# Retention of a two-block transformer layer: centred values, early scores and states, squares on ScalarE, decays inside the stick attention

## The reference

```python
scores = einsum('bhnid,bhnjd->bhnij', qc, kc) * dmat
inner = einsum('bhnij,bhnjd->bhnid', scores, vc)
kv = einsum('bhnjd,bhnje->bhnde', kc * k_dec, vc)
# state n+1 = g_chunk * state n + kv_n, from zero
cross = einsum('bhnid,bhnde->bhnie', qc, state) * q_dec
y = inner + cross
mu, var = mean(y), mean((y - mu) ** 2)      # over the 64 columns of a head
out = ((y - mu) * rsqrt(var + EPS) * gain + bias) * silu(r_g)
```

## Time and profile before

| | us |
|---|---|
| median of 3 runs | 2454.27 (2451.46 to 2454.89) |
| the profiled execution | 2452.69 |
| its span | 2450.8 |

### The profile page before, as it was taken

One profiled execution on the slowest core, in us unless ns is written; L12 is line 12 of the kernel. 1 busy time (PEld: TensorE's weight loads), 2 busy tenths in 40 slices (PEclk: granted clock), 3 DMA queues, 4 the chain that ended last, 5 costly groups with the idle time before them and its releaser, 6 DMA issues.

```text
span 2450.8 us, 30913 instructions
## 1 busy us (share of the span) xinstructions
PE 2273.3 (93%) x10560; PEld 1837.1 (75%) x10560; DVE 1862.5 (76%) x2142; ACT 1397.5 (57%) x1644; POOL 162.9 (7%) x106
## 2 busy tenths in 40 slices
PE   5998888999998998667899999999999999999988
PEld 3866676888787885655588888888888888878866
DVE  7887535556424757565699999999999999999975
ACT  4355524333314336204477778777777778778763
POOL 1000000000000000001001101110110111011010
PEclk8999798999999998678799999999999999999999
DMA  9520313332113210216799999999999999999990
GB/s 326 193 104 14 108 36 102 103 101 79 53 61 116 91 50 1 95 48 242 251 379 375 374 382 375 375 381 375 375 375 381 375 375 381 375 375 377 379 340 35
DMA packets 286881, 571.96 MB, mean 233 GB/s; under 512 B 10556, under 2 KB 35039, under 8 KB 286783
## 3 DMA queue, kind: packets, MB, share of 16 engines
q1 hardware_dynamic: 273615, 523.69, 58.7%
q0 software_dynamic: 13200, 47.38, 6.9%
HBM read 542.71 MB, written 28.32 MB: 233 GB/s over the span
## 4 chain that ended last, share of the span: by engine, by line
PE 57%; SPq 26%; DVE 8%; issue 4%; ACT 3%; DMA 2%; DVEq 0%; ACTq 0%; POOL 0%
SPq L800 25%; PE bank L1793 6%; PE bank L1794 6%; PE bank L1795 6%; PE bank L1443 6%; PE bank L1444 6%; PE bank L1445 6%; PE bank L1642 3%; PE bank L1643 3%; PE bank L1644 3%; PE bank L1424 3%; PE bank L1521 2%; PE bank L1503 1%; SPq L652 1%; DMA x<-in_x 1%
## 5 line engine op out<-in xcount | busy, mean ns | idle before, releaser
L2473 DVE TENSOR_TENSOR w_lo<-stage,w_hi 128x2048 fp32r<-128x2048 f32 x396 | 885.4, 2283 | 5.8 <-ACT w_hi L1258 5.8
L1258 ACT ACTIVATE w_hi<-stage 128x2048 fp32r<-128x2048 f32 x396 | 753.8, 1920 | 197.0 <-DMA stage<-in_w_down 80.4
L1793 PE MATMUL bank<-w_hi,xeT_hi 128*128 128x512 f32 x1056 | 439.2, 416 | 0.0
L1794 PE MATMUL bank<-w_lo,xeT_hi 128*128 128x512 f32 x1056 | 413.3, 391 | 0.0
L1795 PE MATMUL bank<-w_hi,xeT_lo 128*128 128x512 f32 x1056 | 413.3, 391 | 0.0
L1795 PEld LDWEIGHTS bank<-w_hi,xeT_lo 128*128 128x128 f32 x1056 | 199.4, 189 | 42.6
L1794 PEld LDWEIGHTS bank<-w_lo,xeT_hi 128*128 128x128 f32 x1056 | 199.9, 189 | 40.6
L1793 PEld LDWEIGHTS bank<-w_hi,xeT_hi 128*128 128x128 f32 x1056 | 200.5, 190 | 37.4
L1793 PE MATMUL bank<-w_hi,eaT_hi 128*128 128x512 f32 x528 | 209.0, 396 | 4.6 <-DVE eaT_lo L2518 4.6
L1954 DVE TENSOR_TENSOR ring_low<-ring,half_top 128x2048 fp32r<-128x2048 f32 (+2 forms) x42 | 93.1, 2221 | 151.0 <-ACT half_top L994 150.6
L1794 PE MATMUL bank<-w_lo,eaT_hi 128*128 128x512 f32 x528 | 206.1, 390 | 0.0
(11 more groups left out here) (468 smaller groups left out, 3596.4 us busy)
## 6 DMA issues: line engine op xcount, KB each, us to landing
stage<-in_w_up_gate SPq DMA_DIRECT2D x264, 1024.0 KB, 14.0
stage<-in_w_down SPq DMA_DIRECT2D x132, 1024.0 KB, 17.6
ring<-in_w_ada SPq DMA_DIRECT2D x12, 2048.0 KB, 9.4
ring<-in_w_up SPq DMA_DIRECT2D x22, 1024.0 KB, 7.7
ring<-in_w_in SPq DMA_DIRECT2D x10, 2048.0 KB, 7.8
ring<-in_w_out SPq DMA_DIRECT2D x4, 2048.0 KB, 12.8
ring<-in_w_down SPq DMA_DIRECT2D x4, 2048.0 KB, 8.5
stage<-in_w_ple_gate SPq DMA_DIRECT2D x4, 1024.0 KB, 14.5
```

The source lines that it names most:

```text
L1258: fn(w_hi[top_of(h)][:, :], src[:, :], ACT.Copy).then_inc(s_hi, 1)
L1793: mm(bank[b][:, :], hi[:, kk, :], wh[:, k, :], start=bcol is None and kk == 0, stop=False)
L1794: mm(bank[b][:, :], hi[:, kk, :], wl[:, k, :], start=False, stop=False)
L2473: tt(w_lo[h][:, :], stage[h][:, :], w_hi[top_of(h)][:, :].bitcast(FP), ALU.subtract).then_inc(s_lo, 1)
```

## The change

`rv` is centred: each head's mean over its 64 columns is subtracted from the values as soon as they are there, ahead of the stick attention; since outputs and states are linear in the values, the retention's output then has mean zero in each head, and the norm's copy, mean and subtraction go. The off-diagonal zeros of the state come from GpSimd, ahead. The eight decays move from ahead of the stick attention into its steps 1 to 8 on VectorE. There are two tiles of `rS`, three of `state`, two of `gy` and `gsq`. TensorE makes scores two chunks ahead and the key-value products one chunk ahead. ScalarE squares the output straight from the bank. The gain row is multiplied into the gate and the bias row times the gate becomes `gadd`, one chunk ahead (`ret_gate`), so the norm multiplies twice and adds once. ScalarE's two halves of `top` for `wout2` are taken apart, one in chunk 1 and one in chunk 2.

```diff
@@ -215,10 +215,11 @@
+    rS = [at(R + (80 + 6 * i) * KB, [P, H, P], name=f"rS{i}") for i in range(2)]
+    state = [at((24 + 2 * i) * KB, [P, H // 2, 2 * HD], name=f"state{i}") for i in range(3)]
+    gy = [at(R + (20 + 18 * i) * KB, [P, H, HD], name=f"gy{i}") for i in range(2)]
+    gadd = [at(R + (22 + 14 * i) * KB, [P, CW], name=f"gadd{i}") for i in range(2)]
+    gsq = [at(R + (32 + 2 * i) * KB, [P, H, HD], name=f"gsq{i}") for i in range(2)]
@@ -492,13 +493,21 @@
+    def scores_of(n):
+        for j in range(2):
+            product(("rS", n, j), (5 + j) if n % 2 else j)
+    scores_of(0)
+    product(("rkv", 0), 4)
+    scores_of(1)
     for n in range(NT):
-        product(("rS", n, 0), 0); product(("rS", n, 1), 1)
         product(("rO", n), 2 + n % 2)
-        if n < NT - 1:
-            product(("rkv", n), 4)
+        if n < 2:
+            product(("rkv", n + 1), 4)
         if n:
             product(("oT", 3, n - 1), 7)
+        if n < 2:
+            scores_of(n + 2)
@@ -870,6 +879,10 @@
+            full(pool, ("win2", 5, NT - 1))
+            for st in state:
+                for par in range(2):
+                    nc.gpsimd.memset(st[par * HD:(par + 1) * HD, :, (1 - par) * HD:(2 - par) * HD], 0.0).then_inc(s_kz, 1)
@@ -1222,12 +1235,26 @@
+            def ret_square(n):
+                b = full(act_e, ("rO", n))
+                if n >= 2:
+                    act_e.wait_ge(s_ms, 8 + n)
+                fn(gsq[n % 2][:, :, :], b[:, :].rearrange("p (h d) -> p h d", h=H), ACT.Square).then_inc(s_rsq, 1)
+            def ret_root(n):
+                act_e.wait_ge(s_ms, 10 + n)
+                st = hs[:, (9 + n) * 32:(9 + n) * 32 + H]
+                fn(st, st, ACT.Sqrt).then_inc(s_rt, 1)
             for n in range(NT):
-                roots(9 + n)
+                ret_square(n)
                 if n:
                     out_T(3, n - 1)
-                if n == 1:
-                    top(("wout2", 0), 0, 1)
+                ret_root(n)
+                if n in (1, 2):
+                    top(("wout2", 0), n - 1)
@@ -1679,36 +1706,51 @@
-            pe.wait_ge(s_kd, 1)
-            pe.wait_ge(s_rqd, NT)
-            for n in range(NT):
-                c0 = n * P
+            def ret_scores(n):
                 for j in range(2):
                     b = acquire(("rS", n, j))
                     for h in range(j, H, 2):
-                        ins = mm(b[:, h // 2 * P:(h // 2 + 1) * P], half(rT[1], h, c0, P), half(rT[0], h, c0, P), start=True, stop=True)
+                        ins = mm(b[:, h // 2 * P:(h // 2 + 1) * P], half(rT[1], h, n * P, P), half(rT[0], h, n * P, P), start=True, stop=True)
                     publish(ins, ("rS", n, j))
+            def ret_pairs(n):
+                b = acquire(("rkv", n))
+                for j in range(4):
+                    ins = mm(b[:, j * P:(j + 1) * P], rk[:, n, j * P:(j + 1) * P], rv[:, n, j * P:(j + 1) * P], start=True, stop=True)
+                publish(ins, ("rkv", n))
+            def ret_out(n):
                 b = acquire(("rO", n))
                 for j in range(2):
                     taken(pe, ("rS", n, j))
                 if n:
-                    pe.wait_ge(s_st, n)
+                    taken(pe, ("rkv", n - 1))
                 for pair in range(H // 2):
                     if n:
-                        mm(b[:, pair * P:(pair + 1) * P], rqdT[:, pair, c0:c0 + P], state[:, pair, :], start=True, stop=False,
+                        mm(b[:, pair * P:(pair + 1) * P], rqdT[:, pair, n * P:(n + 1) * P], state[n - 1][:, pair, :], start=True, stop=False,
                            skip_group_check=True)
                     for h in (2 * pair, 2 * pair + 1):
-                        ins = mm(b[:, h * HD:(h + 1) * HD], rS[:, h, :], rv[:, n, h * HD:(h + 1) * HD], start=n == 0, stop=True,
+                        ins = mm(b[:, h * HD:(h + 1) * HD], rS[n % 2][:, h, :], rv[:, n, h * HD:(h + 1) * HD], start=n == 0, stop=True,
                                  skip_group_check=True)
                 publish(ins, ("rO", n))
-                if n < NT - 1:
-                    b = acquire(("rkv", n))
-                    for j in range(4):
-                        ins = mm(b[:, j * P:(j + 1) * P], rk[:, n, j * P:(j + 1) * P], rv[:, n, j * P:(j + 1) * P], start=True, stop=True)
...
+            pe.wait_ge(s_kd, NT)
+            pe.wait_ge(s_rqd, NT)
+            pe.wait_ge(s_kz, 10)
+            ret_scores(0)
+            ret_pairs(0)
+            ret_scores(1)
+            for n in range(NT):
+                ret_out(n)
+                if n < 2:
+                    ret_pairs(n + 1)
                 if n:
                     out_T(3, n - 1, o2)
+                if n < 2:
+                    ret_scores(n + 2)
@@ -2378,72 +2420,107 @@
+            for t in range(NT):
+                taken(dve, ("win2", 5, t))
+            rvh = rv[:, :, :].rearrange("p t (h d) -> p (t h) d", d=HD)
+            vmean = hs[:, 4 * 32:5 * 32]
+            link(ve.reduce_sum(vmean, rvh, axis=AX))
+            link(ts(vmean, vmean, 1.0 / HD, None, ALU.mult))
+            link(tt(rvh, rvh, bc(vmean, 2, [P, 32, HD]), ALU.subtract))
             for t in range(NT):
                 full(dve, ("rT", 1, t))
             rk3 = rk[:, :, :].rearrange("p t (h d) -> p t h d", h=H)
             for t in range(NT):
                 taken(dve, ("rT", 0, t))
-                link(tt(rk3[:, t], rk3[:, t], bc(cb("kdec"), 2, [P, H, HD]), ALU.mult))
-                tt(rqdT[:, :, t * P:(t + 1) * P], rT[0][:, :, t * P:(t + 1) * P], blk3(cb("qdec")), ALU.mult).then_inc(s_rqd, 1)
-            dve.wait_ge(s_rqd, NT)
-            dve.nop().then_inc(s_kd, 1)
...
+            def while_sticking(s):
+                if 1 <= s <= NT:
+                    t = s - 1
+                    tt(rk3[:, t], rk3[:, t], bc(cb("kdec"), 2, [P, H, HD]), ALU.mult).then_inc(s_kd, 1)
+                elif NT < s <= 2 * NT:
+                    cols_t = slice((s - NT - 1) * P, (s - NT) * P)
+                    tt(rqdT[:, :, cols_t], rT[0][:, :, cols_t], blk3(cb("qdec")), ALU.mult).then_inc(s_rqd, 1)
+            attention(2, PR2, PT2, o2, while_sticking)
             dmat = cb("dmat").rearrange("p (h i) -> p h i", h=H)
-            for n in range(NT):
+            def ret_mask(n):
                 for j in range(2):
                     label = ("rS", n, j)
                     b = full(dve, label)
-                    if n:
-                        full(dve, ("rO", n - 1))
+                    if n >= 2:
+                        full(dve, ("rO", n - 2))
                     else:
                         full(dve, ("T", 2, 4 * H - 1))
-                    take(tt(rS[:, j::2, :], blk3(b[:, :]), dmat[:, j::2, :], ALU.mult), label)
-                if n < NT - 1:
-                    label = ("rkv", n)
-                    b = full(dve, label)
...
+                    take(tt(rS[n % 2][:, j::2, :], blk3(b[:, :]), dmat[:, j::2, :], ALU.mult), label)
+            def ret_state(n):
+                label = ("rkv", n)
+                b = full(dve, label)
+                if n:
+                    taken(dve, ("rkv", n - 1))
+                for par in range(2):
+                    hp = slice(par * HD, (par + 1) * HD)
+                    src = blk3(b[:, :])[hp, :, par * HD:(par + 1) * HD]
+                    own = state[n][hp, :, par * HD:(par + 1) * HD]
+                    if n == 0:
+                        ins = ve.tensor_copy(own, src)
+                    else:
+                        link(tt(own, state[n - 1][hp, :, par * HD:(par + 1) * HD], bc(cb("gch")[hp, :], 2, [HD, 4, HD]), ALU.mult))
+                        ins = tt(own, src, own, ALU.add)
+                take(ins, label)
+            def ret_gate(n):
+                link(tt(gadd[n % 2][:, :], rg[:, n, :], gnrow[:, 1, :], ALU.mult))
+                link(tt(rg[:, n, :], rg[:, n, :], gnrow[:, 0, :], ALU.mult))
+            def ret_var(n):
+                st = hs[:, (9 + n) * 32:(9 + n) * 32 + H]
+                dve.wait_ge(s_rsq, n + 1)
+                link(ve.reduce_sum(st, gsq[n % 2][:, :, :], axis=AX))
+                ts(st, st, 1.0 / HD, EPS, ALU.mult, ALU.add).then_inc(s_ms, 1)
+            def ret_norm(n):
+                st = hs[:, (9 + n) * 32:(9 + n) * 32 + H]
                 label = ("rO", n)
                 b = full(dve, label)
-                take(ve.tensor_copy(gy[:, :, :], b[:, :].rearrange("p (h d) -> p h d", h=H)), label)
-                taken(dve, label)
-                st = hs[:, (9 + n) * 32:(9 + n) * 32 + 8]
-                link(ve.reduce_sum(st, gy[:, :, :], axis=AX))
...
                 dve.wait_ge(s_rt, 10 + n)
                 link(ve.reciprocal(st, st))
-                link(tt(gy[:, :, :], gy[:, :, :], bc(st, 2, [P, H, HD]), ALU.mult))
-                gf = gy[:, :, :].rearrange("p h d -> p (h d)")
-                link(tt(gf, gf, gnrow[:, 0, :], ALU.mult))
```

(80 more changed lines are left out.)

3 lines of the change are left out of this document (1 added, 2 removed).

## The result

| | before | after |
|---|---|---|
| median, measured side by side | 2454.39 (4 runs, 2451.46 to 2454.89) | 2418.04 (4 runs, 2414.57 to 2419.99) |
| the profiled execution | 2452.69 | 2418.96 |
| its span | 2450.8 | 2416.9 |

The change makes the kernel faster by 36.4 us between these medians; the ratio is 0.9862 with a 95% interval of 0.9849 to 0.9876, that is 30 to 37 us. A second measurement gave 2418.57 against 2450.43, 31.9 us less. The forecast was 28. One of the 17 executions of the kernel before that stand beside the first four experiments took 6470.91 us; the ratios leave it out.

A forecast was written before the change was run, and what follows sets the result against it. The prediction took the retention as a chain alternating between TensorE and VectorE; its walks, with 2.7 us lost in the attention, gave -24.8 to -34.9. It took -28: 2424.7 profiled, 2426.3 as a median, range 2418 to 2434.

The forecast's parts named there:

- the end of the stage sets the rest: Behind the retention: everything later hangs on its last low part, so every us passes to the end one to one.
- The condition on the expert loop: Behind the retention: the forecast is wrong on the rest if the expert loop's length changes by more than 2 us.
- the steps of the retention: Retention: times per instruction group, with output 0 ending at 1005.2 and chunk 0's norm at 1011.0.
- The walk: Retention's new lists on the old time axis, attention loss included: -24.8 slow clock, -29.6 fast behind output 0, -34.9 fast at once.
- when the clock rises: Retention: TensorE, working without a gap, becomes fast around 1005 to 1012 and falls back perhaps once.
- the sum: Whole kernel: 2452.7 profiled less 28 is 2424.7, or 2426.3 as a median.
- rival 2: Retention: TensorE fast at once, by the skill's rule, -34.9 us, median 2419; chance 0.17.
- the decays are a loss inside the attention: Stick attention: of 4.9 us of decays 1.7 are covered and 3.2 not; the attention ends 2.7 us later.
- The 0.5 from the earlier first sigmoid: Ahead of the attention: moving the decays out of VectorE's front lets the first sigmoid start some 0.5 us earlier, at 930.90.
- one table load, behind the first square, at no cost: ScalarE in the retention: one load of 1.28 us, while state 1 (1.8) stands on VectorE; cost 0.
- the folding of the rows: Retention norm: one multiplication behind the root goes, 0.7 per chunk; two gate multiplications, 1.45, come behind the chunk's output.
- whether the centring costs anything: Ahead of the attention: 4.8 us of centring runs where VectorE idled 20.7 us; cost 0.

The follow-up runs named there:

- the first four experiments: Kernel before with decays in attention steps 1 to 8 (2449.53); changed kernel with decays ahead (2422.50); kernel before with new order only (2429.90), new norm only (2436.64).
- wide matmuls: The changed kernel with two extra 128x512 matmuls on TensorE, result unused, into a free bank near the attention's end: 2420.07 in one run.
- six late decays: The changed kernel with six decays in attention steps 33 to 36 and the two that nothing reads left out: 2420.75, ratio 0.9865.

## Why the prediction came out as it did

**Right: the end of the stage sets the rest.** Every kernel's first expert weights were issued 46.3 to 47.9 us after its last low part, and the wait there did not change. While the retention went from 78 to 38 us over the fourteen profiles, the rest stayed between 1376.1 and 1382.3, with nothing changed in it and no trend with the retention, so a us of retention was a us of the total. The condition on the expert loop held: from the second issue of its weights (1177.47 before, 1144.47 after) to the end it took 1273.3 and 1272.4 us.

**Right: the steps of the retention.** Output 0 was to end at 1005.2 and ended at 1004.67; the norm of chunk 0 at 1011.0 and ended at 1010.71; the busy share of VectorE was to be 0.75 and is 34.56 of 47, 0.74. Output to root was to take 1.0 and takes 0.9. The walk gave the stage (from the attention's last copy) 51 us with the slow clock throughout, 46 with the fast one behind output 0, and 41 with the fast one at once. The measured lengths are 47.3 for a slow start that ended at 1017, and 39.4 for a fast one.

**Wrong: when the clock rises.** I had TensorE become fast between 1005 and 1012, after work without a gap. It worked for 24 us without one and stayed at 0.50 all that time. That the rise came at the end of it cost little, because VectorE's list was the bound from there on. And I took the retention's start as slow, as in the one profile I had. It can differ between executions of one program: of the seven profiles with the new order and the new norm and no wide matmuls, four began fast and three slow, and two of these three are the ones with the decays outside the first steps. In the terms of the sum, the retention is 31.1 less than before from a slow start and 39.1 from a fast one; less the 2.1 of the attention, 29.0 and 37.0. The forecast of 28 was the first; rival 2, at 34.9, is the second, and its 0.17 was too small. Its rule, from the Trainium skill, page "TensorE: Matmul & The Clock Gate", section "Why this matters for your kernels", is that sustained work brings the fast clock; the 24 us at 0.50 speak against it. In both executions of the changed kernel TensorE was at 1.00 in the attention's last 7 us; in one the clock fell between 993 and 994, with the retention's first scores, in the other not before 1017, when TensorE had run out of work. The sum met the slow-start value within 1 us although the clock rose 6 to 12 us later than I had it; that is in part luck, since -28 was chosen between two walks.

**Where the 36.4 us come from.** In the profiled pair the span fell by 33.9: 31.1 in the retention and 2.85 in the rest, with 2.1 more ahead of the attention and 2.1 lost in it. The 2.1 ahead and the 2.85 behind are within what these stages vary by. The two measured differences, 36.4 and 31.9, lie between 29 and 37, as a mixture of both starts would; that the timed runs are such a mixture is argued. Only the profiled ones show their clock by stage; the mean granted clocks of the eight timed ones, 0.956 to 0.960, lie about those of the profiled ones with the slow start (0.956) and the fast (0.959).

**Right for the stage, not shown for the kernel: the decays are a loss inside the attention**, by 2.1 us in the stage (68.28 for 66.17), where 2.7 was said. Six profiles with decays in the first steps and no wide matmuls have 68.27 to 68.32, four with the decays elsewhere 65.6 to 66.0, so against these it is 2.3 to 2.7. The 0.5 from the earlier first sigmoid is in it: it now follows its table load at once, as it could have done at 930.90 before. One step with a decay is 1.45 us: VectorE's four instructions and nothing else. In the totals the loss did not appear in any of the three experiments on it: the decays alone cost nothing (at most 1.5 us), and taking them out of the first steps, ahead or late, gave 2422.50 and 2420.75 beside the changed kernel's 2418.04 and 2418.57. The sum took the decays' place and the clock at the retention's start as independent, and that is not shown: by the profiles the fast start, worth 8 us, came only to kernels with the decays in the first steps or with the wide matmuls.

**Right: one table load, behind the first square, at no cost**, with 1.5 us to spare under variance and state.

**Wrong in sign: the folding of the rows.** I counted 0.7 saved in each chunk and called the two gate multiplications, 1.45, work behind the chunk's output. But they stand ahead of the next chunk's masks and variance, and VectorE is the bound there. The walk has them in its times (gate and masks 2.75, 1.45 in chunk 2), so its sum isn't off by them; what was wrong is to take the folding for a gain. Unfolding gave 1.0 to 1.4 us. By VectorE's list, three gates of 1.44 (1029.30 to 1030.74) go, and four multiplications of 0.72 come back: 1.4.

**Not settled:** whether the centring costs anything. The `rT` copies end between 924.1 and 931.3 in kernels with it and at 926.4 to 926.9 in the three without; that scatter hides a us either way. What sets the clock at the retention's start isn't settled either. The run that is missing is the changed kernel with and without the wide matmuls, and with the decays in either place, several times side by side with a profile of each execution.

## What to carry to other kernels

When two engines are each half idle in a stage and take turns, issue the products that depend on nothing one or two rounds ahead, and shorten the chain between them; each alone gave half of the stage's gain or more. Work moved off a critical chain isn't free if it lands ahead of the next link of the same engine: put it where that engine waits for another one, not merely where its result isn't needed yet. The six late decays shortened their stage by 2.7 us in this way, but the kernel's median didn't follow, so a gain read in one stage is to be looked for in the total too. And take two profiles of the same kernel before giving a clock level a role in a sum: here it was worth 8 us and differed between two executions of one program, and perhaps by kernel.

## What the runs showed of the hardware

- TensorE worked 24 us without a gap on matmuls of 64 and 128 columns at granted clock 0.50 (1.2 GHz), and at 1.00 (2.4 GHz) on the same matmuls in another execution of the same program; in the 7 us ahead of them it had been at 1.00 and busy for 6.27 us in both. A group of 16 score matmuls took 3.09 and 1.71 us.
- ScalarE's square and its copy of 128x512 from a bank both take 0.60 us; only the root needed a table load, of 1.28 us, and the squares and copies between roots brought no further one.
